# Expert weights in runs of four light and four heavy units in place of two and two

## The chip, the cores and the metric

The kernel runs on one core of one Trainium2 chip. The metric is the device time of one execution in microseconds; the time of a kernel is the median of its runs. Before the change it is 1384.67 us (three runs, 1384.44 to 1385.2).

## What is computed

Two layers on 256 tokens of width 1024, all in float32: a gated recurrent mixer with a dense SwiGLU, then forgetting attention with a mixture of experts. The change lies in the mixture alone:

```python
logits = (t @ router).astype(jnp.float32)
top_v, top_i = lax.top_k(logits, TOP_K)                  # 2 of 8 experts for each token
w = jax.nn.softmax(top_v, axis=-1)
for e in range(N_EXPERTS):
    out = out + combine[:, e:e + 1].astype(t.dtype) * swiglu(t, w_gate[e], w_up[e], w_down[e])
# swiglu(h, g, u, d) = (silu(h @ g) * (h @ u)) @ d, with g, u of 1024 x 3584 and d of 3584 x 1024
```

Every expert's three matrices (44 MB) are read once from HBM, 352 MB in all.

## The kernel before

**Front part.** The first layer, the attention and the router take about the first 500 us. The change does not reach them.

**Pairs of experts.** The experts are sorted by the number of their tokens and taken in pairs: one with many tokens (the heavy job, 0, up to 128 rows) and one with few (the light job, 1, up to 64 rows). Four pairs run one after the other: two written out, one in a loop, one at the end. The text calls them pair 1 to pair 4.

**Units and loads.** The weights of a pair come in 84 units of 1 MB, one DMA each, numbered 0 to 83 within the pair; load n brings unit n. `pair_table` fixes their order. The 3584 columns are cut into four parts p = 0 to 3 (1024 columns each, the last 512). Part p has a gate stage G and an up stage U (4 units a job, 2 for the last part), and a down stage D of the part before is woven in between in pieces of 2 units a job. The order within a pair is G0, U0, G1, D0, U1, D0, G2, D1, U2, D1, G3, D2, U3, D2, D3. Within each stage `turns` yields first RUN light units, then RUN heavy ones, and so on. PE (`pair`), the loads (`pair_loads`) and the helpers' due points all use this order. Units 16 to 23 are G1, 24 to 27 the first piece of D0, 28 to 35 U1.

**The ring.** The loads go through SP's queue into a ring of ten slots of 1 MB. The slot of unit n is (n + n // 14) % 10: after every 14 units one slot is passed over. So unit 28 takes the slot of unit 19 (nine back), 29 that of 20, 30 that of 21, and so on. Before it issues a load, SP waits until PE has counted up `used` past the unit that had the slot (L431, `sp.wait_ge(used, ...)`, with `last_in_slot`).

**A light unit** is multiplied straight from the ring as it lands (`light_unit`, L1350). **A heavy unit** is first split in two: ACT writes the high half `whi` (L516, three buffers, SPLIT), DVE the low half `lows` (L1490); PE then does twelve 128x512 matmuls, lines L1337, L1338 and L1339 in turn.

**Work that is interleaved by unit number.** ACT and DVE do the splitting in order through `hi_to(n)` and `lo_to(n)`: all heavy units up to number n are split before the program of that engine goes on. Other duties stand between these calls:

```python
# ACT, end of a pair (gathered)
nxt[0] = 0
hi_to(HEAVY[0], following)
gathered_lo(following)
# DVE, end of a pair (finished)
lo_to(HEAVY[0], following)
light_rows(following)          # writes xl, L1967; PE waits for it before unit 0
# DVE, in pair(), p == 0
lo_to(unit("G", 1, 1, 0) + 2, group)
act_T_lo(group, 0)             # aT_lo, L1954; waits for ACT's aT_hi, L778
```

HEAVY[0] is the first heavy unit of a pair. `unit("G", 1, 1, 0)` is the first light unit of G1, number 16. PE transposes the activations of part 0 (`act_transposes`, L1300) after the last light unit ahead of the first heavy unit of G1; ACT then writes `aT_hi` and DVE `aT_lo`. The transposes of the light job (L1307) follow that heavy unit.

Of the kernel before, what the change touches and what calls it, by code (L numbers as in the profile page):

```python
# [48 lines left out]
N_MOE = N_FOXOUT + 4  # L49

PAIR_UNITS = 2 * FFN_UNITS
RING, SPLIT, RUN = 10, 3, 2
SKIP = 14
TURNS = (PAIR_UNITS + PAIR_UNITS // SKIP) // RING
assert TURNS * RING == PAIR_UNITS + PAIR_UNITS // SKIP and FFN_UNITS % SPLIT == 0
# [2013 lines left out]
```

## Time and profile before

| | |
|---|---|
| median of the runs | 1384.67 us |
| the profiled execution | 1385.05 us, span 1383.3 us |
| TensorE busy (PE) | 1335.4 us, 97% |
| VectorE (DVE), ScalarE (ACT) busy | 736.6 us, 53%; 630.2 us, 46% |
| DMA, bytes and mean rate | 434.79 MB, 314 GB/s over the span |
| granted TensorE clock | full (1.00) throughout |

PE's busy time counts a matmul to its modelled end, so 97% does not say that PE could do no more; where it waits is to be read from the waits. The span has a front part of about 500 us at half the DMA rate and the mixture's part of about 880 us at 410 GB/s.

### The profile page before, as it was taken

What the parts mean: (1) busy time and instruction counts of PE and PEld (TensorE: products, weight loads), DVE (VectorE), ACT (ScalarE), POOL (GpSimd) and SP (SyncE); (2) the same over time, 40 slices, a digit from 0 to 9 for tenths busy, and PEclk for the clock granted to TensorE, in tenths of its full rate; (3) what the DMA queues carried; (4) which work ended last, traced back from release to release, by engine and by line L of the source; (5) the groups of instructions that cost most, each with busy time, mean ns of one, the idle gap of its engine ahead of it and who ended that gap; (6) DMA issues with size and microseconds to landing.
All of it is one profiled execution on the core that took longest, in us unless ns stands there. A gap on an engine that the chain in (4) does not pass through costs nothing.

```text
span 1383.3 us, 16134 instructions
## 1 busy us (share of the span) xinstructions
PE 1335.4 (97%) x6427; PEld 939.1 (68%) x6427; DVE 736.6 (53%) x626; ACT 630.2 (46%) x574; POOL 28.9 (2%) x34
## 2 busy tenths in 40 slices
PE   7999999999999989999999999999999999999998
PEld 7978888888888865565565556666556666556665
DVE  6975444446654465554545555544555545445445
ACT  5855344335455344534435344335344345344343
POOL 2000000000300000000000000000000000000000
PEclk9999999999999999999999999999999999999999
DMA  9456555555540049999999999999999999999995
GB/s 335 158 181 220 195 193 184 183 182 161 174 146 7 16 192 410 413 412 414 404 412 410 397 414 412 410 409 409 413 390 412 406 409 411 409 399 414 413 400 242
DMA packets 127882, 434.79 MB, mean 314 GB/s; under 512 B 6960, under 2 KB 9120, under 8 KB 113472
## 3 DMA queue, kind: packets, MB, share of 16 engines
q1 hardware_dynamic: 127344, 433.11, 81.2%
q8 instruction: 51, 0.84, 0.2%
q0 software_dynamic: 368, 0.63, 0.2%
q14 instruction: 23, 0.19, 0.0%
q10 hardware_dynamic: 96, 0.03, 0.0%
HBM read 432.69 MB, written 1.05 MB: 314 GB/s over the span
## 4 chain that ended last, share of the span: by engine, by line
PE 73%; DMA 17%; DVE 5%; ACT 4%; issue 1%; DVEq 0%; SPq 0%; POOL 0%; ACTq 0%
PE ps L1350 15%; PE ps L868 9%; PE ps L870 9%; PE ps L869 9%; PE ps L1337 8%; DMA ring<-in_moe_w_gate_dram 7%; DMA ring<-in_moe_w_up_dram 7%; PE ps L1338 7%; PE ps L1339 7%; DVE lows L1490 3%; ACT whi L516 2%; DMA ring<-in_moe_w_down_dram 1%; PE ps L1269 1%; PE ps L1098 1%; PE ps L1300 1%
## 5 line engine op out<-in xcount | busy, mean ns | idle before, releaser
L1490 DVE TENSOR_TENSOR lows<-ring,whi 128x2048 fp32r<-128x2048 f32 x168 | 383.7, 2291 | 272.6 <-ACT whi L516 272.5
L516 ACT ACTIVATE whi<-ring 128x2048 fp32r<-128x2048 f32 x168 | 320.5, 1912 | 348.0 <-DMA ring<-in_moe_w_up_dram 134.3
L1350 PE MATMUL ps<-ring,xl 128*64 128x512 f32 (+1 forms) x1024 | 204.8, 544 | 5.1 <-DVE xl L1967 5.1
L1483 DVE TENSOR_TENSOR wlo<-raw,whi 128x2048 fp32r<-128x2048 f32 x73 | 166.5, 2288 | 73.5 <-PE ps L870 71.4
L1337 PE MATMUL ps<-whi,hT_hi 128*128 128x512 f32 x448 | 181.3, 405 | 19.9 <-DVE lows L1490 19.8
L509 ACT ACTIVATE whi<-raw 128x2048 fp32r<-128x2048 f32 x73 | 139.3, 1917 | 84.5 <-PE ps L870 82.9
L1338 PE MATMUL ps<-lows,hT_hi 128*128 128x512 f32 x448 | 175.0, 391 | 0.0
L1339 PE MATMUL ps<-whi,hT_lo 128*128 128x512 f32 x448 | 174.7, 390 | 0.0
L868 PE MATMUL ps<-whi,hT_hi 128*128 128x512 f32 x384 | 153.2, 399 | 2.4 <-DVE wlo L1483 1.4
L870 PE MATMUL ps<-whi,hT_lo 128*128 128x512 f32 x384 | 149.8, 390 | 0.0
L869 PE MATMUL ps<-wlo,hT_hi 128*128 128x512 f32 x384 | 149.5, 389 | 0.0
L1350 PEld LDWEIGHTS ps<-ring,xl 128*64 128x64 f32 x1024 | 69.0, 136 | 113.4 <-issue 105.3
L1337 PEld LDWEIGHTS ps<-whi,hT_hi 128*128 128x128 f32 x448 | 84.0, 188 | 77.1 <-issue 31.8
L1350 PE MATMUL ps<-ring,aTl 128*64 128x512 f32 x448 | 102.3, 598 | 0.0
L1339 PEld LDWEIGHTS ps<-whi,hT_lo 128*128 128x128 f32 x448 | 84.1, 188 | 18.3
L1337 PE MATMUL ps<-whi,aT_hi 128*128 128x512 f32 x220 | 90.1, 410 | 5.6 <-DVE lows L1490 5.4
L1338 PEld LDWEIGHTS ps<-lows,hT_hi 128*128 128x128 f32 x448 | 84.2, 188 | 15.4
L1339 PE MATMUL ps<-whi,aT_lo 128*128 128x512 f32 x220 | 86.1, 391 | 0.0
L1338 PE MATMUL ps<-lows,aT_hi 128*128 128x512 f32 x220 | 86.0, 391 | 0.0
L868 PEld LDWEIGHTS ps<-whi,hT_hi 128*128 128x128 f32 x384 | 72.2, 188 | 18.3 <-issue 3.1
L870 PEld LDWEIGHTS ps<-whi,hT_lo 128*128 128x128 f32 x384 | 72.1, 188 | 15.3
L869 PEld LDWEIGHTS ps<-wlo,hT_hi 128*128 128x128 f32 x384 | 72.2, 188 | 13.7
(312 smaller groups left out, 1326.1 us busy)
## 6 DMA issues: line engine op xcount, KB each, us to landing
ring<-in_moe_w_gate_dram SPq DMA_DIRECT2D x112, 1024.0 KB, 13.6
ring<-in_moe_w_up_dram SPq DMA_DIRECT2D x112, 1024.0 KB, 13.7
ring<-in_moe_w_down_dram SPq DMA_DIRECT2D x112, 1024.0 KB, 14.1
raw<-in_fox_w_in_dram SPq DMA_DIRECT2D x16, 1024.0 KB, 5.3
raw<-in_ffn_w_gate_dram SPq DMA_DIRECT2D x14, 1024.0 KB, 5.1
raw<-in_ffn_w_up_dram SPq DMA_DIRECT2D x14, 1024.0 KB, 5.0
raw<-in_ffn_w_down_dram SPq DMA_DIRECT2D x14, 1024.0 KB, 5.1
raw<-in_lru_w_in_dram SPq DMA_DIRECT2D x8, 1024.0 KB, 10.7
```

The lines of the kernel that those rows point to most:

```text
L509: nc.scalar.activation(whi[:, m % HR], raw[:, m % RR], ACT.Copy).then_inc(hi_done, 1)
L516: nc.scalar.activation(whi[:, 1 + q % SPLIT], ring[:, slot(i)], ACT.Copy).then_inc(hi_done, 1)
L868: mm(dst(t), hi, whi[:, m % HR, k * CW:(k + 1) * CW], start=first and k == 0, stop=False)
L869: mm(dst(t), hi, wlo[:, m % LR, k * CW:(k + 1) * CW], start=False, stop=False)
L870: ins = mm(dst(t), lo, whi[:, m % HR, k * CW:(k + 1) * CW], start=False, stop=last and k == UK - 1)
L1098: ins = mm(dst, qT[rows, c, qs], kT[rows, c, 0:w], start=False, stop=True, skip_group_check=True)
L1337: mm(ps[:, bank + h], hi, w_hi[:, cols], start=first and k == 0, stop=False)
L1338: mm(ps[:, bank + h], hi, w_lo[:, cols], start=False, stop=False)
L1339: ins = mm(ps[:, bank + h], lo, w_hi[:, cols], start=False, stop=last and k == tiles - 1)
L1350: ins = mm(ps[g * HD:(g + 1) * HD, bank, 0:half], src(k), ring[:, slot(i), cols], start=first and k == 0, stop=last and k == tiles - 1, sk ...
L1483: nc.vector.tensor_tensor(wlo[:, m % LR], raw[:, m % RR], whi[:, m % HR].bitcast(F32), ALU.subtract).then_inc(lo_done, 1)
L1490: nc.vector.tensor_tensor(lows[:, slot(i)], ring[:, slot(i)], whi[:, 1 + q % SPLIT].bitcast(F32), ALU.subtract).then_inc(lo_done, 1)
```

## The change

One constant is changed. `RUN` is the length of a run in `turns`; the slots, the number of buffers and the `hi_to` and `lo_to` calls keep their text.

```diff
-RING, SPLIT, RUN = 10, 3, 2
+RING, SPLIT, RUN = 10, 3, 4
```

A stage of 4 units a job had the order light, light, heavy, heavy, light, light, heavy, heavy (LLHHLLHH). It now has LLLLHHHH. These are the six stages G0, U0, G1, U1, G2 and U2 of each pair. The D pieces, G3 and U3 have 2 units a job and stay as they are. HEAVY[0] goes from unit 2 to unit 4; the heavy units of G1 go from 18, 19, 22, 23 to 20, 21, 22, 23.

DVE in the second pair, from U0's last product (`gt`, L1949) through the accumulation of the first pair's output (`X`) and `aT_lo` to the splitting in G1 and after; before:

```order
L1949 TENSOR_TENSOR gt<-gt,ps 128x1024
L1490 TENSOR_TENSOR lows<-ring,whi 128x2048
L1943 TENSOR_TENSOR X<-ps,X 128x2x512
L1954 TENSOR_TENSOR aT_lo<-ps,aT_hi 128x1024
L1490 TENSOR_TENSOR lows<-ring,whi 128x2048 x9
```

and with the change:

```order
L1949 TENSOR_TENSOR gt<-gt,ps 128x1024
L1943 TENSOR_TENSOR X<-ps,X 128x2x512
L1954 TENSOR_TENSOR aT_lo<-ps,aT_hi 128x1024
L1490 TENSOR_TENSOR lows<-ring,whi 128x2048 x8
```

Before, one heavy unit of G1 (18) was split ahead of `aT_lo`; now all four stand behind it.

PE at the same place, from the last scatter matmuls (L1269) through the light units of G1 and the eight transposes to the first heavy unit; before:

```order
L1269 MATMUL ps<-hT_lo,ST 128x512
L1350 MATMUL ps<-ring,xl 64x512 x8
L1300 MATMUL ps<-ident,gt 128x128 x8
L1337 MATMUL ps<-whi,hT_hi 128x512
L1338 MATMUL ps<-lows,hT_hi 128x512
```

and with the change:

```order
L1269 MATMUL ps<-hT_lo,ST 128x512
L1350 MATMUL ps<-ring,xl 64x512 x16
L1300 MATMUL ps<-ident,gt 128x128 x8
L1337 MATMUL ps<-whi,hT_hi 128x512
L1338 MATMUL ps<-lows,hT_hi 128x512
```

Four light units stand ahead of the transposes in place of two.

DVE at the boundary between pair 1 and pair 2, from the last `aT_lo` of pair 1; before:

```order
L1954 TENSOR_TENSOR aT_lo<-ps,aT_hi 128x512
L1490 TENSOR_TENSOR lows<-ring,whi 128x2048 x3
L1967 TENSOR_TENSOR xl<-ps,xl 128x512
L1490 TENSOR_TENSOR lows<-ring,whi 128x2048
L1935 SCALAR_TENSOR_TENSOR yl_lo<-ps,weight,yl_hi 128x512
```

and with the change:

```order
L1954 TENSOR_TENSOR aT_lo<-ps,aT_hi 128x512
L1490 TENSOR_TENSOR lows<-ring,whi 128x2048 x3
L1967 TENSOR_TENSOR xl<-ps,xl 128x512
L1935 SCALAR_TENSOR_TENSOR yl_lo<-ps,weight,yl_hi 128x512
L1490 TENSOR_TENSOR lows<-ring,whi 128x2048
```

Three units are split ahead of `xl` in both. The third of them is HEAVY[0] of the next pair, which was its unit 2 and is now its unit 4.

## Rows read from the trace of the kernel before

**Rows 1.** The page: DMA in 40 slices, chain by engine, PE's busy time.

```profile
PE 1335.4 (97%) x6427; PEld 939.1 (68%) x6427; DVE 736.6 (53%) x626; ACT 630.2 (46%) x574; POOL 28.9 (2%) x34
...
DMA  9456555555540049999999999999999999999995
...
PE 73%; DMA 17%; DVE 5%; ACT 4%; issue 1%; DVEq 0%; SPq 0%; POOL 0%; ACTq 0%
```

**Rows 2.** Busy time by stretch, 600 to 700 us; last: clock, DMA share, GB/s.

```profile
600.00:700.00 100.00, 94.85 (x451) 58.81 (x449) 50.03 (x26) 42.49 (x28) 0.00 (x0) 1.00 1.03 409
```

**Rows 3.** Waits of PE, 484 us to the end: total, times, longest.

```profile
PE ps L1337 <- DVE lows L1490: 25.2, 29, 1.8
PE ps L1350 <- DVE xl L1967: 5.1, 4, 1.5
```

**Rows 4.** Timeline, SP's queue around 787 and 1004 us: start, duration.

```profile
787.63 0.38 SPq L432 DMA_DIRECT2D ring<-in_moe_w_up_dram  x1
...
1004.44 0.38 SPq L432 DMA_DIRECT2D ring<-in_moe_w_up_dram  x1
```

**Rows 5.** DMA view of those two issues: KB each, microseconds to landing.

```profile
ring<-in_moe_w_up_dram SPq DMA_DIRECT2D x1, 1024.0 KB, 6.5
...
ring<-in_moe_w_up_dram SPq DMA_DIRECT2D x1, 1024.0 KB, 5.5
```

**Rows 6.** The ring's view, 484 us to the end, its last line.

```profile
DMA to landing us min/median/max: 5.2/13.8/19.6
```

**Rows 7.** Timeline, ACT, DVE and PE at the start of pair 2.

```profile
726.44 1.92 ACT L516 ACTIVATE whi<-ring 128x2048 fp32r<-128x2048 f32 x1 [4.27 <-DMA ring<-in_moe_w_gate_dram]
736.66 1.92 ACT L516 ACTIVATE whi<-ring 128x2048 fp32r<-128x2048 f32 x1 [4.01 <-DMA ring<-in_moe_w_gate_dram]
...
728.39 2.29 DVE L1490 TENSOR_TENSOR lows<-ring,whi 128x2048 fp32r<-128x2048 f32 x1 [3.89 <-ACT whi L516]
730.60 0.68 DVE L1967 TENSOR_TENSOR xl<-ps,xl 128x512 f32<-128x512 f32 x1
...
731.54 3.65 PE L1350 MATMUL ps<-ring,xl 128*64 128x512 f32 x16 [1.48 <-DVE xl L1967]
735.12 0.50 PE L1337 MATMUL ps<-whi,hT_hi 128*128 128x512 f32 x1
...
740.79 1.08 PE L1350 MATMUL ps<-ring,xl 128*64 128x512 f32 x4
```

**Rows 8.** Timeline, PE, ACT and DVE in G1 of pair 2.

```profile
778.79 1.23 PE L1300 MATMUL ps<-ident,gt 128*128 128x128 f32 x8
784.59 0.50 PE L1337 MATMUL ps<-whi,hT_hi 128*128 128x512 f32 x1 [1.33 <-DVE lows L1490]
787.53 3.22 PE L1350 MATMUL ps<-ring,xl 128*64 128x512 f32 x14
...
780.05 1.03 ACT L778 ACTIVATE aT_hi<-ps 128x1024 fp32r<-128x1024 f32 x1 [2.22 <-PE ps L1300]
...
781.11 1.23 DVE L1954 TENSOR_TENSOR aT_lo<-ps,aT_hi 128x1024 fp32r<-128x1024 f32 x1 [3.89 <-ACT aT_hi L778]
782.25 2.28 DVE L1490 TENSOR_TENSOR lows<-ring,whi 128x2048 fp32r<-128x2048 f32 x1
```

**Rows 9.** Timeline, ACT: unit 34 of pair 2, units 2 and 34 of pairs 3 and 4.

```profile
809.47 1.92 ACT L516 ACTIVATE whi<-ring 128x2048 fp32r<-128x2048 f32 x1 [4.08 <-DMA ring<-in_moe_w_up_dram]
...
943.32 1.92 ACT L516 ACTIVATE whi<-ring 128x2048 fp32r<-128x2048 f32 x1 [4.31 <-DMA ring<-in_moe_w_gate_dram]
...
1026.90 1.92 ACT L516 ACTIVATE whi<-ring 128x2048 fp32r<-128x2048 f32 x1 [4.76 <-DMA ring<-in_moe_w_up_dram]
...
1159.57 1.92 ACT L516 ACTIVATE whi<-ring 128x2048 fp32r<-128x2048 f32 x1 [4.26 <-DMA ring<-in_moe_w_gate_dram]
...
1244.04 1.92 ACT L516 ACTIVATE whi<-ring 128x2048 fp32r<-128x2048 f32 x1 [5.69 <-DMA ring<-in_moe_w_up_dram]
```

## The prediction

> **What bounds the kernel now.** I read the page first. PE is busy for 97% and takes 73% of the chain, so it looks like the bound [rows 1]. The DMA slices say something else: from the fifteenth slice to the end every slice has a 9. The mixture's part starts there. A stretch within it, 600 to 700 us, gives a DMA share of 1.03 at 409 GB/s with the full TensorE clock [rows 2]. PE does wait there, though for little at a time: 29 waits for `lows` with 25.2 us in all, and one wait for `xl` in each of the four pairs, 5.1 us in all [rows 3]. These are the waits of an engine that has caught up with its supply. So the mixture's part is bound by the DMA stream: 84 loads a pair, one after the other. Between the landings of units 2 and 6 of pair 2, read off ACT's starts at 726.44 and 736.66, there are 10.22 us, or 2.555 us a load [rows 7].
>
> A late PE therefore costs nothing, up to the point where its slots come free too late and the stream runs dry. How far is that? Issue to landing takes 13.8 us in the median and 5.2 at the least [rows 6]; a load needs 2.555 of that for its own bytes. So most loads have 8 us of cover and some have none. The thin place is unit 28, which takes the slot of unit 19. In pair 2 it is issued at 787.63, when PE has finished unit 19, and lands 6.5 us later. In pair 3 (1004.44) it takes 5.5 us, next to the least there is [rows 4 to 6]. So at this place of each later pair the cover is 1.3 us or less, and whatever makes units 19 to 22 later goes into the time. Pair 1 starts with a full ring and is not at risk.
>
> **The change part by part.** The same instructions run and the same bytes move. Only waits and their order change.
>
> *Fewer switches on PE.* Two light units take 3.58 us (731.54 to 735.12) and two heavy ones in one run 5.67 (735.12 to 740.79) [rows 7]. A heavy unit that opens a run takes 2.94 (784.59 to 787.53) [rows 8], so the second takes 2.73: opening a run costs 0.21 us. A light run opens with about as much (the two light units are 1.9 and 1.7). A stage of LLLLHHHH has one switch pair less: 0.4 us of PE time.
>
> *Start of a pair.* PE starts unit 0 when DVE has written `xl`, and ahead of `xl` DVE splits HEAVY[0]. In pair 2 that unit lands at 726.44, its `lows` run from 728.39, `xl` follows at 730.60 and PE starts at 731.54 [rows 7]. HEAVY[0] is now unit 4 and lands two loads later, 2 x 2.555 = 5.1 us. ACT and DVE are idle for 4 us ahead of it in these rows, so nothing absorbs that. PE starts unit 0 at 736.65. From there to G1 PE works without a wait in pair 2, so it stays 5.1 late, less what the switches give.
>
> *G1.* PE's transposes start at 778.79. ACT's `aT_hi` (780.05), DVE's `aT_lo` (781.11) and one `lows` (782.25) follow one another, and PE starts the next heavy unit at 784.59: 5.80 us after the transposes [rows 8]. Before, unit 18 had been split earlier and ran beneath that chain, and the light transposes with it. Now no unit of G1 is split before `aT_lo`, so the first heavy unit, 20, waits for the whole chain and PE stands idle for 4.6 us in place of 1.33.
>
> The times in pair 2 are then: transposes at 778.79 + 5.1 (late start) + 3.4 (two further light units at 1.7) - 0.8 (two stages of fewer switches) = 786.5. Unit 19, now light, is finished by then, and load 28 goes out at 786.5 in place of 787.6: no loss there. Unit 20 runs from 786.5 + 5.8 = 792.3 to 795.2. Load 29 waits for it. With 5.3 us to landing, between the 5.2 of an empty queue and the 5.5 of pair 3, it lands at 800.5. Unit 21 comes 0.5 (the light transposes) and 2.9 us later, at 798.6: load 30 lands at 803.9. Units 22 and 23 come at 2.73 each, so loads 31 and 32 land at 806.7 and 809.4. Load 33 waits for a light unit and is covered again; load 34 lands two loads later, at 814.5.
>
> Now the stretch between the landings of units 2 and 34, whose ends can be read in all three pairs. With the change it is 814.5 - 726.4 = 88.1 us, and it is set by PE, so it is the same in each of them. Before it was 83.0 in pair 2, 83.6 in pair 3 and 84.5 in pair 4 [rows 7, 9]. The change costs 5.1 + 4.5 + 3.6 = 13.2 us. The remaining 50 or so loads of a pair run at the stream's rate in both kernels, since PE catches up at 2.3 us a unit against 2.56. Pair 1, the front part and the end after the last load stay.
>
> One unknown comes on top. 32 loads at 2.555 are 81.8 us, and the three stretches before take 1.2, 1.8 and 2.7 more, 5.7 in all: the stream has slow landings now and then. Where they fall while the queue is dry they vanish in my 88.1; where they fall behind load 29 they add to it. So the sum lies between 13.2 and 18.9 us. I take 1.5 of the 5.7, as most of the stretch lies ahead of load 29: **14.7 us**.
>
> The Trainium skill, "DMA: Bandwidth & Descriptors", in its account of what a DMA costs, gives about 2.0 us fixed plus the bytes at 436 GB/s, which makes 4.4 us for 1 MB as an estimate. This case's trace does not agree: its shortest is 5.2 us [rows 6]. By the page's figure each late load would land 0.9 us earlier and the sum would be 12.0 us; the rows decide, and the sum stands.
>
> **The rivals.**
> 1. *The dry queue costs more than its gap.* The pairs whose load 28 was nearest to the least time have the longest stretches (84.5 and 83.6 against 83.0), so running dry may itself bring slow landings of 1 to 1.5 us. The new gaps are longer. With 2 us more in each pair the sum is 19 to 24 us: 1404 to 1409.
> 2. *Only the late start reaches the stream.* If DVE's chain in G1 were hidden (say hidden behind the lateness that PE has already), unit 20 would end 3.3 us earlier, and each pair would lose up to 3.3 us less: 13.2 - 9.9 = 3.3, with the slow landings 3 to 5, or about 1389. For it speaks nothing but that the cover may be larger than I read; against it, unit 28's 5.5 us [rows 5].
> 3. *No change.* If load 29 had 4 us more of cover than I count, the stream would never notice: 1384.7. The 6.5 and 5.5 us speak against it.
> 4. *Faster: PE is the bound after all.* Then only the switches count: 0.4 x 6 stages x 4 pairs = 9.6 us, which gives 1375. The page's 97% and the 73% of the chain [rows 1] speak for it. It decides only if the DMA share falls clearly under 1 in the mixture's part; the 1.03 [rows 2] is against.
>
> **How the numbers follow.** The profiled execution took 1385.05 us, 0.4 above the median of the runs, 1384.67. 1385.05 + 14.7 = 1399.8 for a profiled run, 1399.4 against the median. Chances: the forecast with its own range of 1395 to 1403, 0.65; rival 1, 0.15; rival 2 and anything that costs 2 to 10 us, 0.12; no change, 0.04; faster, 0.04. Differences within 0.2% (2.8 us) can't be told from none. Slower is then 0.92, no change 0.04, faster 0.04. The range leaves out the last two and the lower part of rival 2, and of rival 1 the upper half: 1390 to 1406.
>
> **What would show it.** In the changed kernel's profile: PE's wait for `xl` is about 6.6 us in each of pairs 2 to 4, 20 us in all in place of 5.1, and the first heavy unit of G1 has 4 to 5 us of idle time, released by `lows`, right behind `aT_lo`. Load 29 of these pairs takes 5.2 to 5.5 us to land and comes some 4 us after load 28's landing and the usual 2.56. DMA busy stays the same in total, while the share falls in one slice of each later pair. The stretch from unit 2 to unit 34 is 88 us. I am wrong if load 29 takes 8 us or more (cover is left: rival 3), if the stretches exceed 90 (rival 1), or if PE's wait for `xl` is short because DVE reaches it earlier.

## The result

| | before | changed |
|---|---|---|
| median of the runs | 1384.93 us | 1420.11 us (1416.64 to 1421.13) |
| ratio | | 1.0249, 95% interval 1.0236 to 1.0261 |
| profiled execution, span | 1383.3 us | 1419.4 us |
| mean granted TensorE clock | 1.000 | 0.979 |

The kernel is 35 us slower. The forecast was 1399.4 with a range to 1406: the right sign, and less than half of the size.

From the page of the changed kernel: PE's busy time, and the clock, DMA share and rate in 40 slices.

```profile
PE 1343.3 (95%) x6427; PEld 951.2 (67%) x6427; DVE 735.3 (52%) x626; ACT 630.3 (44%) x574; POOL 28.9 (2%) x34
...
PEclk9999999999999999999999999998999998999999
DMA  9456565555520089999999899999899999989995
GB/s 335 168 181 210 181 199 185 178 184 175 176 89 1 16 338 411 392 413 409 406 410 376 323 412 415 401 414 365 346 372 412 407 411 394 361 315 416 415 400 243
```

Against [rows 1], the DMA slices now have one slice under 9 in each later pair (323, 346 and 315 GB/s, where the stream's rate is 410), and the clock line, full before, has two slices of 8. The waits of PE from 484 us to the end (total, times, longest):

```profile
PE ps L1337 <- DVE lows L1490: 37.8, 24, 6.9
PE ps L1350 <- DVE xl L1967: 20.4, 4, 6.6
```

These answer to [rows 3]. The wait for `xl` went from 5.1 to 20.4 us, 6.6 the longest: the number forecast. The one for `lows` has a longest of 6.9 us. It stands in G1 of pair 1; the timeline of PE, ACT and DVE there (start, duration; idle before and who ended it):

```profile
562.22 1.23 PE L1300 MATMUL ps<-ident,gt 128*128 128x128 f32 x8
570.39 0.79 PE L1337 MATMUL ps<-whi,hT_hi 128*128 128x512 f32 x1 [6.94 <-DVE lows L1490]
570.98 0.63 PE L1338 MATMUL ps<-lows,hT_hi 128*128 128x512 f32 x1
571.41 0.63 PE L1339 MATMUL ps<-whi,hT_lo 128*128 128x512 f32 x1
...
564.05 1.91 ACT L516 ACTIVATE whi<-ring 128x2048 fp32r<-128x2048 f32 x1 [0.65 <-DMA ring<-in_moe_w_gate_dram]
565.87 1.01 ACT L778 ACTIVATE aT_hi<-ps 128x1024 fp32r<-128x1024 f32 x1
...
566.91 1.22 DVE L1954 TENSOR_TENSOR aT_lo<-ps,aT_hi 128x1024 fp32r<-128x1024 f32 x1 [10.38 <-ACT aT_hi L778]
568.05 6.68 DVE L1490 TENSOR_TENSOR lows<-ring,whi 128x2048 fp32r<-128x2048 f32 x3
```

Two things are to be seen. The transposes end at 563.5, but ACT writes `aT_hi` only at 565.87: it first splits unit 22, whose load has just landed at 564.05. And behind PE's idle time the matmuls stand 0.43 us apart (570.98, 571.41) where heavy matmuls elsewhere stand 0.23 apart. Stretches of 2 us in G1 of pair 3 tell why (busy time of PE, PEld, DVE, ACT, POOL; clock; DMA share; GB/s):

```profile
1020.00:1022.00 2.00, 0.00 (x0) 0.00 (x0) 1.52 (x2) 0.44 (x1) 0.00 (x0) 1.00 1.02 418
1022.00:1024.00 2.00, 0.05 (x1) 0.05 (x1) 2.00 (x2) 0.00 (x0) 0.00 (x0) 0.60 0.86 344
1024.00:1026.00 2.00, 2.00 (x5) 1.61 (x6) 2.00 (x1) 0.00 (x0) 0.00 (x0) 0.50 0.09 37
1026.00:1028.00 2.00, 2.00 (x7) 1.52 (x6) 2.00 (x2) 0.00 (x0) 0.00 (x0) 0.50 0.00 0
1028.00:1030.00 2.00, 2.00 (x10) 1.56 (x9) 0.30 (x1) 0.56 (x1) 0.00 (x0) 0.69 0.00 0
1030.00:1032.00 2.00, 2.00 (x10) 1.62 (x9) 0.61 (x1) 2.00 (x3) 0.00 (x0) 1.00 0.61 156
```

PE is idle until 1023.95. In that time the clock falls to 0.50, its lower level of 1.2 GHz, and stays there for most of the first heavy unit behind the idle time. The last two columns show the price: the DMA engines stand still while PE works through unit 20 at half speed, since load 29 waits for that unit's slot. SP's queue and the DMA view for loads 28 and 29 of this pair:

```profile
1018.27 0.38 SPq L432 DMA_DIRECT2D ring<-in_moe_w_up_dram  x1
...
1029.44 0.38 SPq L432 DMA_DIRECT2D ring<-in_moe_w_up_dram  x1
```

```profile
ring<-in_moe_w_up_dram SPq DMA_DIRECT2D x1, 1024.0 KB, 7.8
...
ring<-in_moe_w_up_dram SPq DMA_DIRECT2D x1, 1024.0 KB, 5.1
```

Load 28 lands at 1026.1, load 29 at 1034.5: 8.4 us later where the stream's step is 2.56. The same fall of the clock stands at the start of the pair. PE's first light units of pair 3, and the stretches around them:

```profile
965.27 10.02 PE L1350 MATMUL ps<-ring,xl 128*64 128x512 f32 x32 [6.61 <-DVE xl L1967]
```

```profile
962.00:964.00 2.00, 0.00 (x0) 0.00 (x0) 1.86 (x1) 2.00 (x4) 0.00 (x0) 0.50 1.01 403
...
968.00:970.00 2.00, 2.00 (x8) 0.61 (x6) 2.00 (x2) 0.20 (x1) 0.00 (x0) 0.50 1.03 410
970.00:972.00 2.00, 2.00 (x8) 0.53 (x6) 1.28 (x1) 0.00 (x0) 0.00 (x0) 0.70 0.98 338
```

Four light units take 10.0 us here, and 7.1 at the full clock (in the run with constant matmuls below).

The late start also empties the queue once ahead of G1. Load 17 waits for unit 8; in pair 2 it is issued at 763.92, and this is its time to landing, with the stretch behind its issue:

```profile
ring<-in_moe_w_gate_dram SPq DMA_DIRECT2D x1, 1024.0 KB, 5.2
```

```profile
764.00:765.00 1.00, 1.00 (x8) 0.42 (x6) 1.00 (x1) 1.00 (x1) 0.00 (x0) 1.00 0.24 57
```

In pair 3 it takes 5.0 us. In the kernel before, load 17 took 11.4, 10.0 and 9.9 us in pairs 2 to 4.

Last, the ends of the stretches that the prediction was made of. In the changed kernel the first heavy unit is 4 (5.1 us behind unit 2); these are ACT's starts for units 4 and 34 of pairs 2, 3 and 4:

```profile
734.46 1.91 ACT L516 ACTIVATE whi<-ring 128x2048 fp32r<-128x2048 f32 x1 [9.38 <-DMA ring<-in_moe_w_gate_dram]
821.21 1.91 ACT L516 ACTIVATE whi<-ring 128x2048 fp32r<-128x2048 f32 x1 [0.67 <-PE ps L1350]
960.20 1.91 ACT L516 ACTIVATE whi<-ring 128x2048 fp32r<-128x2048 f32 x1 [9.42 <-DMA ring<-in_moe_w_gate_dram]
1049.64 1.91 ACT L516 ACTIVATE whi<-ring 128x2048 fp32r<-128x2048 f32 x1 [0.67 <-DMA ring<-in_moe_w_up_dram]
1188.88 1.91 ACT L516 ACTIVATE whi<-ring 128x2048 fp32r<-128x2048 f32 x1 [9.43 <-DMA ring<-in_moe_w_gate_dram]
1278.48 1.91 ACT L516 ACTIVATE whi<-ring 128x2048 fp32r<-128x2048 f32 x1 [0.64 <-DMA ring<-in_moe_w_up_dram]
```

With 5.1 us added, unit 2 to unit 34 takes 91.9, 94.5 and 94.7 us. Forecast were 88.1 in each; before it was 83.0, 83.6 and 84.5 [rows 7, 9]. These stretches hold 8.9 + 10.9 + 10.2 = 30.0 of the 36.1 us by which the spans differ. Pair 1 holds 2.9, by the landing of its last load. The rest, 3.2 us, is almost all behind unit 34 of pairs 3 and 4: from there to the last landing the stream takes 126.4 and 126.2 us, in place of 125.0 and 124.6.

### The profile page after: what moved, and what is told of

It is laid out like the page before. It is cut to its first block, busy times and chain, and to the rows that moved or that the text cites. A ratio compares the mean times of both kernels' runs of the same rounds, so it can differ in the third digit from the quotient of the medians.

```text
span 1419.4 us, 16138 instructions
## 1 busy us (share of the span) xinstructions
PE 1343.3 (95%) x6427; PEld 951.2 (67%) x6427; DVE 735.3 (52%) x626; ACT 630.3 (44%) x574; POOL 28.9 (2%) x34
## 4 chain that ended last, share of the span: by engine, by line
PE 70%; DMA 16%; DVE 6%; ACT 4%; SPq 2%; issue 1%; DVEq 0%; POOL 0%; ACTq 0%
PE ps L1350 14%; PE ps L868 8%; PE ps L1337 8%; PE ps L870 8%; PE ps L869 8%; DMA ring<-in_moe_w_gate_dram 8%; PE ps L1338 8%; PE ps L1339 8%; DMA ring<-in_moe_w_down_dram 5%; DMA ring<-in_moe_w_up_dram 3%; DVE lows L1490 3%; ACT whi L516 2%; SPq L432 2%; PE ps L1269 1%; DVE wlo L1483 1%
## 5 line engine op out<-in xcount | busy, mean ns | idle before, releaser
L1350 PE MATMUL ps<-ring,xl 128*64 128x512 f32 (+1 forms) x1024 | 206.8, 558 | 20.4 <-DVE xl L1967 20.4
L1337 PE MATMUL ps<-whi,hT_hi 128*128 128x512 f32 x448 | 183.2, 409 | 33.3 <-DVE lows L1490 33.2
L1338 PE MATMUL ps<-lows,hT_hi 128*128 128x512 f32 x448 | 178.8, 399 | 0.0
L1339 PE MATMUL ps<-whi,hT_lo 128*128 128x512 f32 x448 | 178.5, 398 | 0.0
L509 ACT ACTIVATE whi<-raw 128x2048 fp32r<-128x2048 f32 x73 | 139.4, 1916 | 85.5 <-PE ps L870 82.9
L1350 PEld LDWEIGHTS ps<-ring,xl 128*64 128x64 f32 x1024 | 73.1, 140 | 140.8 <-issue 132.7
L870 PE MATMUL ps<-whi,hT_lo 128*128 128x512 f32 x384 | 149.8, 390 | 0.0
L1337 PEld LDWEIGHTS ps<-whi,hT_hi 128*128 128x128 f32 x448 | 86.5, 193 | 72.4 <-DVE lows L1490 35.5
L1339 PEld LDWEIGHTS ps<-whi,hT_lo 128*128 128x128 f32 x448 | 86.5, 193 | 19.1
L1338 PEld LDWEIGHTS ps<-lows,hT_hi 128*128 128x128 f32 x448 | 86.5, 193 | 16.8
L1337 PE MATMUL ps<-whi,aT_hi 128*128 128x512 f32 x220 | 90.2, 410 | 4.8 <-DVE lows L1490 4.6
L1339 PE MATMUL ps<-whi,aT_lo 128*128 128x512 f32 x220 | 86.1, 391 | 0.0
L1338 PE MATMUL ps<-lows,aT_hi 128*128 128x512 f32 x220 | 86.0, 391 | 0.0
L870 PEld LDWEIGHTS ps<-whi,hT_lo 128*128 128x128 f32 x384 | 72.1, 188 | 15.4
```

The lines of the kernel that those rows point to most:

```text
L509: nc.scalar.activation(whi[:, m % HR], raw[:, m % RR], ACT.Copy).then_inc(hi_done, 1)
L870: ins = mm(dst(t), lo, whi[:, m % HR, k * CW:(k + 1) * CW], start=False, stop=last and k == UK - 1)
L1337: mm(ps[:, bank + h], hi, w_hi[:, cols], start=first and k == 0, stop=False)
L1338: mm(ps[:, bank + h], hi, w_lo[:, cols], start=False, stop=False)
L1339: ins = mm(ps[:, bank + h], lo, w_hi[:, cols], start=False, stop=last and k == tiles - 1)
L1350: ins = mm(ps[g * HD:(g + 1) * HD, bank, 0:half], src(k), ring[:, slot(i), cols], start=first and k == 0, stop=last and k == tiles - 1, sk ...
```

## Experiments

Three causes are to be told apart: the wait at a pair's start, the chain in G1, and TensorE's clock behind both. Each edit is to the changed kernel (RUN = 4), unless said otherwise. Medians are given; before is 1384.6 to 1384.93 in the same sessions.

**xl first.** The wait at the start is taken away.

```diff
-                hi_to(HEAVY[0], following)
                 gathered_lo(following)
+                hi_to(HEAVY[0], following)
...
-                lo_to(HEAVY[0], following)
                 light_rows(following)
+                lo_to(HEAVY[0], following)
```

> RUN = 4 as in the changed kernel, but xl (and ACT's low half of the gathered rows) is written before the first heavy unit of the next pair is split, so that PE need not wait for unit 4's landing at the start of a pair. What the changed kernel does in G1 stays. Theory (the two waits add up to empty the queue, and each lets TensorE's clock fall): PE's wait for xl goes from 20.4 us to nearly 0, the clock stays full at the starts of the pairs, pair 1 still loses its 3 us, and in pairs 2 to 4 load 29 is late by 1 to 3 us each: 1388 to 1396. Rival (the G1 chain alone is the cost, the start is hidden): 1412 or more. Rival (the start alone is the cost): 1385.

Measured: 1392.37 us, ratio 1.0054 (1.0038 to 1.0071). One of the two waits is gone and with it 28 of the 35 us. What is left in G1, on PE in pair 2 and in two stretches there:

```profile
787.39 0.79 PE L1337 MATMUL ps<-whi,hT_hi 128*128 128x512 f32 x1 [4.57 <-DVE lows L1490]
```

```profile
786.00:788.00 2.00, 0.61 (x2) 0.52 (x3) 2.00 (x2) 0.00 (x0) 0.00 (x0) 0.50 0.99 414
788.00:790.00 2.00, 2.00 (x6) 1.62 (x5) 2.00 (x2) 0.00 (x0) 0.00 (x0) 0.50 1.02 418
```

The idle time of 4.6 us is the one forecast, and the clock falls in it.

**Unit 20 split first.** The chain in G1 gets its cover back.

```diff
-                        hi_to(unit("G", 0, 1, 0) + 2, group)
+                        hi_to(unit("G", 0, 1, 0) + 1, group)
                         act_T_hi(group, 0)
...
-                        lo_to(unit("G", 1, 1, 0) + 2, group)
+                        lo_to(unit("G", 0, 1, 0), group)
                         act_T_lo(group, 0)
```

> RUN = 4, but in G1 the first heavy unit (20) is split by DVE before aT_lo, and ACT splits only units 20 and 21 before aT_hi, so that PE has unit 20 to work on while the chain runs. The start of a pair stays as in the changed kernel. Theory: pair 1 loses nothing, the idle time of 7 us in G1 falls under 3 us and the clock stays full there, but the start still costs 6.6 us of wait and 2 to 3 us of slow clock a pair: 1398 to 1406. Rival (the start is hidden): 1385. Rival (the G1 chain is not the cost): 1415 or more.

Measured: 1401.0 us, ratio 1.0116 (1.0099 to 1.0133). The waits for `xl` stay at 20.3 us. Either edit alone takes away more than half of the loss (28 and 19 of 35). With G1's wait alone left 7.6 us are lost, with the start's alone 16.2; that makes 23.8, and the two together cost 35.2. So the waits are not a sum of two prices: they draw on one cover. The start's wait empties the queue by itself: load 30 takes 5.1, 5.0 and 5.3 us to land in pairs 2 to 4, though unit 20 has no long wait ahead of it.

**Both edits.**

> RUN = 4 with both edits: xl before the next pair's first split, and unit 20 split before aT_lo. Theory: nothing of the changed kernel's loss is left, and load 28 is no longer late either: 1381 to 1385, with the full clock and no landing gap over 5 us in the mixture's part. Rival (runs of four cost something of their own, such as the stream's slow landings or a longer wait of each first heavy unit): 1390 or more.

Measured: 1381.5 us, ratio 0.9976 (0.9966 to 0.9986). Nothing of the loss is left, and 3 us are won over the kernel before. In this run load 28 of pairs 2 to 4 takes 14 us to land; in the kernel before it took 5.5 to 6.5. The clock was not full throughout, as had been expected: it falls to 0.50 three times in the mixture's part (from 519, 1086 and 1301 us), and the time does not show it, since the loads have their cover.

**Constant matmuls in the idle places.** Waits and splits as in the changed kernel, but TensorE is kept at work. The results go to PSUM banks that are free at that point and are not read.

```diff
+            def fill(bank, count):
+                for n in range(count):
+                    mm(ps[:, bank, 0:T], ident_r[:], mask_r[:], start=True, stop=True, skip_group_check=True)
...
+                if group is not OPENING:
+                    fill(3, 55)
...
                             act_transposes(group, 0)
+                            fill(7, 36)
```

> The changed kernel with matmuls on constants whose results nobody reads put into PE's two idle places: 36 of 128x256 after the eight transposes of G1 (about 4.3 us) and 55 at the start of pairs 2 to 4 (about 6.6 us). Waits and splits stay as in the changed kernel. Theory (TensorE's clock falls to its lower level after the idle time, and the heavy and light units behind it run slow while the stream is already dry): the granted clock is 1.00 throughout, the mixture's first heavy unit in G1 takes 2.7 us in place of 5, and the time is 1420 less about 14, 1403 to 1410. Rival (the clock is a symptom and the units would be late anyway): 1417 to 1422.

Measured: 1405.51 us, ratio 1.0148 (1.0131 to 1.0165). PE in G1 of pair 2:

```profile
790.74 4.55 PE L1373 MATMUL ps<-mask_r,ident_r 128*128 128x256 f32 x36
795.56 0.50 PE L1337 MATMUL ps<-whi,hT_hi 128*128 128x512 f32 x1 [0.27 <-DVE lows L1497]
796.38 0.40 PE L1337 MATMUL ps<-whi,hT_hi 128*128 128x512 f32 x1
...
797.07 0.39 PE L1337 MATMUL ps<-whi,hT_hi 128*128 128x512 f32 x1
```

The useful matmuls start no earlier: 5.8 us after the transposes, as before. But from 796.38 to 797.07 there are three of them (L1337, L1338, L1339), 0.69 us, so they are 0.23 apart, the full clock. Unit 20 ends 69.1 us after the landing of unit 2 in each of pairs 2 to 4, by the issue of load 29; in the changed kernel it was 72.1, 74.4 and 74.5. Holding the clock there gives 14.6 us back. In G1 of pair 1 the wait is longer than the constant matmuls, PE is idle for 2.6 us behind them, and the clock still falls for 3.4 us:

```profile
572.00:574.00 2.00, 2.00 (x6) 1.52 (x5) 2.00 (x2) 0.00 (x0) 0.00 (x0) 0.50 1.03 430
```

**The kernel before with xl first** (RUN = 2, the first edit).

> The kernel before (RUN = 2) with xl written before the next pair's first heavy unit is split. Theory (all that the before kernel lost to late loads is the dry spot at load 28 of pairs 2 to 4, which the shorter lateness removes): 1381 to 1383.5, the same as RUN = 4 with both edits (1381.5), so that the length of the run is worth nothing by itself. Rival (fewer switches on PE or later slots make runs of four better by themselves): 1384 or more, clearly above 1381.5.

Measured: 1381.93 us, ratio 0.9978 (0.9969 to 0.9987). It is within 0.5 us of RUN = 4 with both edits (1381.5), so the length of the run is worth next to nothing by itself. The stretches from unit 2 to unit 34 take 82.8 to 82.9 us in pairs 2 to 4, in place of 83.0, 83.6 and 84.5 [rows 7, 9]: the slow landings at loads 29 and 30 are gone.

**xl first, and constant matmuls in G1** (RUN = 4).

> RUN = 4 with xl written first (as in the run that took 1392.4) and 36 constant matmuls after G1's transposes, so that the wait in G1 stays but TensorE has work during it. Theory (what is left in that run is the clock: 2 us a pair at the slow level on top of a wait that the ring would cover): the clock stays full in G1, load 28 and 29 are covered in pairs 2 to 4, and the time is 1383 to 1387. Rival (the wait itself is what costs, with the clock as a bystander): 1390 to 1393.

Measured: 1385.03 us, ratio 0.9998 (0.9988 to 1.0007). A stretch in G1 of pair 2 (786 to 788 us):

```profile
786.00:788.00 2.00, 1.73 (x12) 1.39 (x11) 2.00 (x2) 0.00 (x0) 0.00 (x0) 1.00 1.03 430
```

The chain in G1 of pairs 2 to 4 is as long as before, and it costs nothing: the ring covers it. Of the 7.6 us that were left with xl first, 7.3 were the clock's.

**One ACT call shortened** (in G1 only unit 20 is split before `aT_hi`, DVE unchanged).

```diff
-                        hi_to(unit("G", 0, 1, 0) + 2, group)
+                        hi_to(unit("G", 0, 1, 0), group)
                         act_T_hi(group, 0)
```

> The changed kernel with one ACT call shortened: only unit 20 (not 20 to 22) is split into whi before aT_hi in G1. Theory (in pair 1 aT_hi stands behind the landing of unit 22, while in pairs 2 to 4 those units have landed long before): pair 1's first heavy unit of G1 follows the light ones by about 9 us in place of 13.4 and pair 1 loses 0 to 1.5 us in place of 3; the other pairs keep their 8 to 12 us: 1415 to 1419. Rival (pair 1's loss comes from DVE's order alone): 1420 as the changed kernel.

Measured: 1417.96 us, ratio 1.0235 (1.0219 to 1.025). The idle time in pair 1 is now that of the other pairs:

```profile
567.89 0.80 PE L1337 MATMUL ps<-whi,hT_hi 128*128 128x512 f32 x1 [4.57 <-DVE lows L1490]
```

It was 6.94. The clock still falls, so unit 20 ends 10.6 us after unit 19, not 9; but the last load of pair 1 lands 0.3 us later than in the kernel before, in place of 2.9.

**Constant matmuls and the shortened ACT call.**

> The changed kernel with the two places of constant matmuls (which held the clock and gave 1405.5) and the shortened ACT call (only unit 20 split before aT_hi, which took pair 1's loss away). What is left is what the prediction summed: the two waits of pairs 2 to 4 at the full clock. Theory (the three causes add up: late loads as forecast, the clock, pair 1): the pairs 2 to 4 lose 5 to 6.5 us each, pair 1 nothing, 1400 to 1404. Rival (the waits in pair 1 and the clock overlap with something else): still 1405 or more.

Measured: 1403.76 us, ratio 1.0137 (1.012 to 1.0154). This is the case that the prediction had summed up: the two waits of pairs 2 to 4 at the full clock, and pair 1 all but untouched (its last load lands 0.4 us later than before). Unit 20 ends 69.1 to 69.2 us after the landing of unit 2 in pairs 2 to 4; forecast was 68.8. Load 29 of pair 2 takes 7.6 us from issue to landing here, though no other load is in flight when it goes out; in pairs 3 and 4 it takes 5.1 and 5.3:

```profile
ring<-in_moe_w_up_dram SPq DMA_DIRECT2D x1, 1024.0 KB, 7.6
```

## Why the prediction was wrong

**What bounds the kernel: right.** The stream of loads does, and a late PE costs nothing until a slot comes free too late. With the chain in G1 whole and the start freed, at the full clock, the time is that of the kernel before (1385.03). Load 28, with 1.3 us of cover or less, was a thin place, and freeing it gives 3 us over the kernel before with either length of run. It was not the only one: load 17 of pairs 3 and 4 took 10.0 and 9.9 us to land, so against the least of 5.2 a start 5.1 us later leaves it no cover. "Most loads have 8 us of cover" passed over that.

**Fewer switches on PE: right, worth nothing.** RUN = 4 and RUN = 2 with their waits removed are at 1381.5 and 1381.93. PE's busy time is 1331.1 us in the first and 1335.2 in the second; the stream decides, and PE's 4 us don't reach the time. This closes rival 4.

**Start of a pair: right in the wait, wrong in what follows it.** 6.6 us were forecast and measured. The step that failed is "From there to G1 PE works without a wait in pair 2, so it stays 5.1 late": it took every unit's duration at the full clock. The four light units behind the idle time took 10.0 us in pair 3 in place of 7.1. Unit 19 ended 61.8, 63.2 and 63.3 us after the landing of unit 2 in pairs 2 to 4, by the issue of load 28; forecast was 60.1.

**G1: the same step.** The chain of 5.80 us and the idle time of 4.6 us came as forecast. "Unit 20 runs from 792.3 to 795.2" did not: in pair 3 it ran from 1023.95 to 1029.4, 5.5 us in place of 2.9. That is why the stretches came out at 91.9 to 94.7 us. Over 90 had been named as the sign of rival 1, but the run with constant matmuls brings unit 20 back to 69.1 us after unit 2: most of the excess is PE's, and not that of a dry queue.

So the term that was missing is TensorE's clock. [Rows 2] says 1.00, and I carried that over to a kernel with idle times that the kernel before never had: its longest wait is 1.8 us [rows 3], the new ones are 4.6 and 6.6. The Trainium skill, "TensorE: Matmul & The Clock Gate", section "HAM oscillation", says that a matmul kernel which waits long enough before each tile lets the clock gate close and starts every tile cold. The traces agree: the clock is 0.50 behind 4.6 and 6.6 us of idle time, here at two places of a pair and not at every tile. I had not weighed it. Holding the clock takes 14.6 us off the changed kernel (1420.11 to 1405.51), and 7.3 off the one with xl first.

**Pair 1: wrong.** "Pair 1 starts with a full ring and is not at risk" looked at the ring only. In pair 1 ACT runs close behind the landings, and its `hi_to(... + 2)` puts `aT_hi` behind the landing of unit 22: 6.9 us of idle time, a fall of the clock, and load 29 late. The shortened ACT call takes 2.6 of pair 1's 2.9 us away; on the whole time it is worth 2.2 us, and 1.75 with the constant matmuls.

**The sum for what was left: low.** The last run has only the forecast causes in it and is at +19.2 us against the 1384.6 of its session, with 14.7 forecast and 18.9 as the upper bound. By the landings of the last loads, pairs 2 to 4 lose 5.9, 6.6 and 5.7 us; forecast were 5.1, 4.5 and 3.6. PE's times fit within 0.4 us. The mis-sized term is the slow landings, of which I had taken 1.5 us: in that run unit 2 to unit 34 takes 88.9 to 89.8 us, so 0.8 to 1.7 us came on top of 88.1 in each pair, 4.2 in all. In pair 2 it is one load: load 29 took 7.6 us where 5.3 had been put. Rival 1 had this part, but the clock made more of the miss.

**The account.** Taken off in this order, of 35.2 us 14.6 go with the clock in the idle places, 1.75 with the shortened ACT call, and 18.8 are left for the two waits at the full clock through late loads, where 14.7 had been forecast. In another order the shares would differ: with `xl` first the clock was worth 7.3. Why loads land slowly now and then stays open. In the two runs whose stream never ran dry (both edits; the kernel before with `xl` first) pairs 2 to 4 have just one step over 3.1 us each, of 3.9 to 4.0 us at loads 16 to 19; the runs that ran dry have up to eight in a pair, part of them set by late issues. That a dry spell brings them on is not shown: no run separates it.

## What to carry to other kernels

Duties that are interleaved by unit number ("split up to n, then do this") change their meaning when the order of the units changes: after reordering, work out for each such call what now stands ahead of the duty, and whether that has landed. When a change makes new idle time on TensorE, read how long it is and price what comes behind it at the lower clock, above all where a transfer waits for just that unit. Two waits can draw on one cover and cost more together (35.2 us here) than the sum of each left alone (7.6 and 16.2), so removing one of them does not show its share.

## What the hardware showed

- After 4.6 us of idle time the granted clock was 0.50, and a heavy unit of twelve matmuls took 5.0 to 5.5 us, 2.7 at the full clock. No wait of up to 1.8 us in the kernel before did that. With both edits there is an idle time of 2.4 to 2.6 us in the middle of each pair: in pairs 3 and 4 the clock fell to 0.50 about 1 us after the work went on (from 1086 and 1301 us), in pairs 1 and 2 it stayed at 1.00.
- The 36 constant matmuls of 128x256 took 4.55 us, 0.12 each with the modelled end of the last, and held the clock at 1.00 over the same wait in pairs 2 to 4.
- With no other load in flight, load 29 of pairs 2 to 4 (1 MB) took 4.9, 5.1 and 5.2 us from issue to landing in the changed kernel. In both runs with constant matmuls at the two places, that of pair 2 took 7.6; no cause is known.
- Load 18 of pair 2 was issued 1.7 us behind load 17 and landed 4.2 us after it, though its own time from issue was 7.7 us and the queue had all but run dry; the stream's usual step is 2.56. I had not expected a gap there, and have no cause for it.
